# Moving activation tiles by 32 to 192 bytes against the weights in SBUF, in a chain of nine blocks whose matmuls read float32r operands

## The chip, the core and the metric

The kernel runs on one NeuronCore of one Trainium2 chip. The metric is the device time of one execution in microseconds (us), the median of three runs.

## The reference

A sequence of 256 tokens of width 1024 goes through two layers of a first model and one layer of a second, all in float32:

```
for i in range(2):
    x = x + 0.5 * swiglu(rms_norm(x, ffn1_norm[i]), w_gate[i], w_up[i], w_down[i])   # width 2816
    h = rms_norm(x, mix_norm[i])
    x = x + (moba_mixer(h, ...) if i == 0 else mamba2_mixer(h, ...))
    x = x + 0.5 * swiglu(rms_norm(x, ffn2_norm[i]), w_gate2[i], w_up2[i], w_down2[i])

def swiglu(x, w_gate, w_up, w_down):
    return (jax.nn.silu(x @ w_gate) * (x @ w_up)) @ w_down

# second model
h = rms_norm_2(x, norm_g) * (1.0 + scale) + shift
proj = h @ w_in                        # 1024 x 9216, then two gated recurrences
x = x + gate * (m @ w_out)
return rms_norm_2(x, final_g)
```

Almost all of the work is a product of 256 tokens with weight matrices that are read once.

## The kernel before

Every weight matrix comes in units of 128 x 2048 float32 (8 KB in each of 128 partitions). A ring of three slots, `raw`, takes them from HBM. ScalarE copies a unit to `w_hi` as float32r (`split_hi`, L390), and VectorE writes the rest, raw minus `w_hi`, to `w_lo` (`split_lo`, L402). Activations are split in the same way. A product is then three float32r matmuls into one accumulator: activation hi by weight hi, activation hi by weight lo, activation lo by weight hi. The units follow one another in one order through all stages, and semaphores (`hi_ready`, `lo_ready`, `unit_used`) hand the slots on.

A matmul on TensorE has two operands in SBUF. The stationary one (128 x 128) is loaded into the array first, with an instruction of its own in the trace (LDWEIGHTS, engine PEld), and the moving one (128 x 256 or 128 x 512) streams through it. The load for the next matmul runs while the present one streams.

- In the four feed-forward blocks, gate and up (L705, L712, L718) have the normed input `hT` as the stationary operand and `w_hi` or `w_lo` as the moving one. Down (L735 to L737, L750 to L752) has the hidden activations as the stationary operand: `hidT_hi` and `hidT_lo` for chunks with an even number, `odd_hidT_hi` and `odd_hidT_lo` for odd ones.
- The projections of attention (L438, L439, L445), of the z part of the second mixer (L1510 to L1512) and most of those of the second model (L2003 to L2005) also hold `hT` and move the weights.
- Where the output is wanted turned, the weights are the stationary operand and `hT` moves, 256 columns wide (L473, L475, L481, L509) or 512 (L504, L1462).
- The three output projections hold `oT`, `yT` and `mT` (L1159 to L1163, L438 to L445, L2031 to L2053). Their tiles lie in the work region and keep their distance from the weights modulo 256 bytes.

Tiles get their addresses by hand. `keep` puts one tile behind the other from the start of SBUF, each rounded up to 64 bytes, and `region` gives a second allocator that starts at a given offset:

```
x = keep("x", [P, TT, D])
hT = keep("hT", [P, KD, 2, SEQ], R32)
...
WORK = -(-top[0] // 128) * 128
```

Within the tiles all steps between operands are multiples of 512 bytes (a tile `hT[:, k, part, t*128:...]` starts at 2048 k + 1024 part + 512 t), but for L1462, whose stationary tiles are 256 bytes apart.

Of the kernel before, what the change touches and what calls it, by code (L numbers as in the profile page):

```python
# [144 lines left out]
def build(nc, w, out):  # L145
    with ExitStack() as ctx:
# [19 lines left out]
        top = [-(-nc.sbuf_base // 64) * 64]  # L166

        def at(offset, name, shape, dt=F32):
            t = nc.alloc_sbuf_tensor_at(name, shape, dt, offset=offset)
            size = int(np.prod(shape[1:])) * 4  # L170
            assert offset + size <= nc.sbuf_usable_end, (name, offset + size - nc.sbuf_usable_end)
            return t, offset + -(-size // 64) * 64

        def keep(name, shape, dt=F32):
            t, top[0] = at(top[0], name, shape, dt)
            return t

        def region(start):

            end = [start]  # L180

            def take(name, shape, dt=F32):
                t, end[0] = at(end[0], name, shape, dt)
                return t

            return take, end

        x = keep("x", [P, TT, D])
        hT = keep("hT", [P, KD, 2, SEQ], R32)
        hT_hi, hT_lo = hT[:, :, 0, :], hT[:, :, 1, :]  # L190
        raw = keep("raw", [P, SLOTS, UNIT])
        w_hi = keep("w_hi", [P, SLOTS, UNIT], R32)
# [1 line left out]
        ffn_tiles = top[0]  # L194
        silu_g = keep("silu_g", [P, TT, FC])
        hid = keep("hid", [P, TT, FC])
        hidT_hi = keep("hidT_hi", [P, 2, SEQ], R32)
        hidT_lo = keep("hidT_lo", [P, 2, SEQ], R32)
        const1 = keep("const1", [P, FIRST_W])
        cols = keep("cols", [P, P])  # L200
        taps = keep("taps", [P, P])
# [10 lines left out]
        WORK = -(-top[0] // 128) * 128  # L212
# [12 lines left out]


        start, start_end = region(WORK + 8192)
        rows_in = start("rows_in", [P, P])
        taps_in = start("taps_in", [P, P])
# [4 lines left out]
        trig = start("trig", [P, 2, TT, HALF])  # L234

        norm, _ = region(WORK)
        xn = norm("xn", [P, TT, D])
        ffn, _ = region(WORK + 7 * 8192)
        hidT = ffn("hidT", [P, 2, SEQ])
        hidT_parts = ((hidT_hi, hidT_lo), (ffn("odd_hidT_hi", [P, 2, SEQ], R32), ffn("odd_hidT_lo", [P, 2, SEQ], R32)))  # L240


# [8 lines left out]
        late, _ = region(late_start)  # L251
# [38 lines left out]
        head_rows, _ = at(r2_end[0] - 4 * SEQ, "head_rows", [P, SEQ])  # L290
        step_rows, _ = at(r2_end[0] - 8 * SEQ, "step_rows", [2 * SH, 2 * SEQ])
# [2417 lines left out]
```

How the kernel before makes its waits and increments, by code:

```python
            def order(*instructions):  # L158
                for i in instructions:
                    i.then_inc(sem(name), 1)
                counts[name] = counts.get(name, 0) + len(instructions)
                engine.wait_ge(sem(name), counts[name])
# [205 lines left out]
        def load_unit(sp, unit, halves, step=0, per=0):  # L368
            n, slot, turn = place(unit, step, per)
            if unit >= SLOTS:
                sp.wait_ge(sem("lo_ready"), n - (SLOTS - 1))
            for dst, src in halves:
                sp.dma_start(dst, src).then_inc(sem(f"landed_{slot}"), 16)
# [5 lines left out]
        def split_hi(act, unit, step=0, per=0):  # L379
            if unit >= UNITS:
                return
            n, slot, turn = place(unit, step, per)
            act.wait_ge(sem(f"landed_{slot}"), 16 * PARTS * (turn + 1))
            if unit >= SLOTS:
                act.wait_ge(sem("unit_used"), n - (SLOTS - 1))
            to, src = w_hi[:, slot, :], raw[:, slot, :]
            if unit == FIRST_UNIT["ssm_dt"]:
                to, src = (step_weights(part, slot)[:, :, 0:SH] for part in (w_hi, raw))
            act.activation(to, src, ACT.Copy).then_inc(sem("hi_ready"), 1)
# [1 line left out]
        def split_lo(dve, unit, step=0, per=0):  # L392
            if unit >= UNITS:
                return
            n, slot, _ = place(unit, step, per)
            dve.wait_ge(sem("hi_ready"), n + 1)
            to, src, hi = w_lo[:, slot, :], raw[:, slot, :], w_hi[:, slot, :]
            if unit == FIRST_UNIT["ssm_dt"]:
```

## Time and profile before

| what | value |
| --- | --- |
| time, median of 3 runs | 1321.93 us (1321.92 to 1321.98) |
| the profiled execution's own time | 1321.68 us |
| its span, first to last instruction | 1319.9 us |
| TensorE busy | 1308.6 us, 99% of the span |
| VectorE busy | 1079.1 us, 82% |
| ScalarE busy | 713.6 us, 54% |
| matmuls | 7751 |
| moved from HBM | 252 MB, 192 GB/s over the span |

The busy time of a matmul in the trace runs from its start to its modelled end, and matmuls overlap in it: the mean of 389 ns for one is not what it costs in a stream. What it costs is the distance between the starts of two that follow one another, and that is read from the timeline.

### The profile page before, as it was taken

The numbers are of one execution on the slowest core, as the hardware profiler recorded it, in microseconds if no ns is written. First come the engines' busy times: TensorE is split into PE (matmuls) and PEld (weight loads), VectorE is DVE, ScalarE is ACT, GpSimd is POOL, SyncE is SP. The second block draws the span as 40 slices with busy tenths as digits, with TensorE's granted clock in tenths as the row PEclk, the third lists the DMA queues.
The fourth block names the chain that finished last, engine by engine and source line by source line (L and its number), as shares of the span: only waits on it lengthen the run. The fifth ranks groups of instructions, "written<-read, shape, count | busy, mean of one in ns | idle before, by whom it ended". The sixth has DMA issues, their size and how long they took to land.

```text
span 1319.9 us, 20183 instructions
## 1 busy us (share of the span) xinstructions
PE 1308.6 (99%) x7751; PEld 1105.4 (84%) x7751; DVE 1079.1 (82%) x1592; ACT 713.6 (54%) x840; POOL 205.1 (16%) x193
## 2 busy tenths in 40 slices
PE   9999999999999999999999999999999999999998
PEld 7888888888888888888899988888888888888886
DVE  6977788868999789998786999769777767878587
ACT  6444455665444454444465688854444466558553
POOL 2400001102000010000000035200000001654940
PEclk9999999999999999999999999999999999999999
DMA  8655556528577654876544565475655555654541
GB/s 274 223 191 191 191 179 204 191 77 306 192 260 267 242 186 146 269 233 222 184 160 155 175 215 180 145 257 166 210 194 196 197 171 160 200 172 143 175 152 56
DMA packets 158445, 254.29 MB, mean 193 GB/s; under 512 B 8800, under 2 KB 99248, under 8 KB 156704
## 3 DMA queue, kind: packets, MB, share of 16 engines
q1 hardware_dynamic: 155136, 232.68, 53.0%
q0 software_dynamic: 2576, 18.45, 4.0%
q10 hardware_dynamic: 656, 2.11, 0.4%
q8 instruction: 52, 0.85, 0.3%
q14 instruction: 25, 0.20, 0.0%
HBM read 252.12 MB, written 1.08 MB: 192 GB/s over the span
## 4 chain that ended last, share of the span: by engine, by line
PE 97%; DVE 1%; issue 1%; ACT 1%; DMA 0%; SPq 0%; POOLq 0%; POOL 0%; DVEq 0%; ACTq 0%
PE psum L718 12%; PE psum L712 12%; PE psum L705 12%; PE psum L736 6%; PE psum L737 5%; PE psum L735 5%; PE psum L2003 4%; PE psum L2004 4%; PE psum L2005 4%; PE psum L438 3%; PE psum L439 3%; PE psum L445 3%; PE psum L473 2%; PE psum L481 2%; PE psum L475 2%; PE psum L504 2%
## 5 line engine op out<-in xcount | busy, mean ns | idle before, releaser
L390 ACT ACTIVATE w_hi<-raw 128x2048 fp32r<-128x2048 f32 (+1 forms) x220 | 419.7, 1910 | 316.5 <-PE psum L718 121.0
L402 DVE TENSOR_TENSOR w_lo<-raw,w_hi 128x2048 fp32r<-128x2048 f32 x219 | 506.8, 2335 | 99.7 <-ACT w_hi L390 98.2
L839 DVE STREAM_TRANSPOSE hidT<-hid 32x128 f32<-32x128 f32 x704 | 213.2, 303 | 22.1
L705 PE MATMUL psum<-w_hi,hT 128*128 128x512 f32 x704 | 174.5, 390 | 0.1
L718 PE MATMUL psum<-w_lo,hT 128*128 128x512 f32 x704 | 173.9, 389 | 0.0
L712 PE MATMUL psum<-w_hi,hT 128*128 128x512 f32 x704 | 173.9, 389 | 0.0
L705 PEld LDWEIGHTS psum<-w_hi,hT 128*128 128x128 f32 x704 | 131.8, 188 | 27.9 <-ACT w_hi L1009 0.8
L712 PEld LDWEIGHTS psum<-w_hi,hT 128*128 128x128 f32 x704 | 132.1, 188 | 27.5
L718 PEld LDWEIGHTS psum<-w_lo,hT 128*128 128x128 f32 x704 | 132.1, 188 | 27.4
L786 ACT ACTIVATE silu_g<-psum,rstd 128x256 f32<-128x256 f32 x88 | 37.0, 472 | 113.5 <-PE psum L718 107.9
L2003 PE MATMUL psum<-w_hi,hT 128*128 128x512 f32 x224 | 88.7, 396 | 0.0
L2005 PE MATMUL psum<-w_hi,hT 128*128 128x512 f32 x224 | 87.3, 390 | 0.0
L2004 PE MATMUL psum<-w_lo,hT 128*128 128x512 f32 x224 | 87.3, 390 | 0.0
L473 PE MATMUL psum<-hT,w_hi 128*128 128x256 f32 x256 | 62.6, 285 | 0.0
L737 PE MATMUL psum<-w_hi,odd_hidT_lo 128*128 128x512 f32 x160 | 62.2, 389 | 0.0
L735 PE MATMUL psum<-w_hi,hidT_hi 128*128 128x512 f32 x160 | 62.2, 389 | 0.0
L736 PE MATMUL psum<-w_lo,hidT_hi 128*128 128x512 f32 x160 | 62.2, 389 | 0.0
L737 PE MATMUL psum<-w_hi,hidT_lo 128*128 128x512 f32 x160 | 62.2, 389 | 0.0
L735 PE MATMUL psum<-w_hi,odd_hidT_hi 128*128 128x512 f32 x160 | 62.2, 389 | 0.0
L736 PE MATMUL psum<-w_lo,odd_hidT_hi 128*128 128x512 f32 x160 | 62.2, 389 | 0.0
L475 PE MATMUL psum<-hT,w_lo 128*128 128x256 f32 x256 | 62.1, 283 | 0.0
L830 DVE TENSOR_TENSOR hid<-psum,silu_g 128x512 f32<-128x512 f32 x44 | 30.3, 689 | 36.9 <-ACT silu_g L786 36.9
(407 smaller groups left out, 2180.6 us busy)
## 6 DMA issues: line engine op xcount, KB each, us to landing
raw<-in_ffn_w_down SPq DMA_DIRECT2D x88, 512.0 KB, 5.2
raw<-in_ffn_w_gate SPq DMA_DIRECT2D x87, 512.0 KB, 4.1
raw<-in_ffn_w_up SPq DMA_DIRECT2D x87, 512.0 KB, 5.3
raw<-in_w_in SPq DMA_DIRECT2D x72, 512.0 KB, 4.6
raw<-in_ssm_w_in SPq DMA_DIRECT2D x48, 512.0 KB, 4.6
raw<-in_attn_w_qkv SPq DMA_DIRECT2D x24, 512.0 KB, 4.8
ada_in<-in_w_ada POOLq DMA_DIRECT2D x8, 1536.0 KB, 7.2
raw<-in_ssm_w_out SPq DMA_DIRECT2D x16, 512.0 KB, 4.4
```

The source lines that it names most:

```text
L390: act.activation(to, src, ACT.Copy).then_inc(sem("hi_ready"), 1)
L402: dve.tensor_tensor(to, src, hi.bitcast(F32), ALU.subtract).then_inc(sem("lo_ready"), 1)
L705: pe.matmul(psum[:, banks[t], :], hT_hi[:, k, t * P:(t + 1) * P], hi[:, kk, :], start=k == 0, stop=False)
L712: pe.matmul(psum[:, banks[t], :], hT_lo[:, k, t * P:(t + 1) * P], hi[:, kk, :], start=False, stop=False)
L718: m = pe.matmul(psum[:, banks[t], :], hT_hi[:, k, t * P:(t + 1) * P], lo[:, kk, :], start=False, stop=k == KD - 1)
L735: pe.matmul(to, a, hi[:, k, cs], start=start and k == 0, stop=False)
L736: pe.matmul(to, a, lo[:, k, cs], start=False, stop=False)
L737: m = pe.matmul(to, b, hi[:, k, cs], start=False, stop=False)
L839: dve.transpose(to[:, :, :, 32 * a:32 * (a + 1)], src[:, :, :, 32 * b:32 * (b + 1)])\
L2003: pe.matmul(to, a, hi[:, kk, :], start=k == 0, stop=False)
L2004: pe.matmul(to, a, lo[:, kk, :], start=False, stop=False)
L2005: m = pe.matmul(to, b, hi[:, kk, :], start=False, stop=k == KD - 1)
```

## The change

The change moves no instruction and no wait: on each of the five engines the instructions before and after are the same and in the same order. Only addresses differ. Three gaps are put between tiles that stand one behind the other, and one in the work region (`skip` is new and raises the allocator's top):

```
+        def skip(size):
+            top[0] += size
+
...
         x = keep("x", [P, TT, D])
+        skip(64)
         hT = keep("hT", [P, KD, 2, SEQ], R32)
+        skip(192)
         hT_hi, hT_lo = hT[:, :, 0, :], hT[:, :, 1, :]
         raw = keep("raw", [P, SLOTS, UNIT])
         w_hi = keep("w_hi", [P, SLOTS, UNIT], R32)
...
         hid = keep("hid", [P, TT, FC])
+        skip(32)
         hidT_hi = keep("hidT_hi", [P, 2, SEQ], R32)
         hidT_lo = keep("hidT_lo", [P, 2, SEQ], R32)
+        skip(224)
         const1 = keep("const1", [P, FIRST_W])
...
-        ffn, _ = region(WORK + 7 * 8192)
+        ffn, ffn_end = region(WORK + 7 * 8192)
         hidT = ffn("hidT", [P, 2, SEQ])
+        ffn_end[0] += 192
         hidT_parts = ((hidT_hi, hidT_lo), (ffn("odd_hidT_hi", [P, 2, SEQ], R32), ffn("odd_hidT_lo", [P, 2, SEQ], R32)))
```

The byte offsets in a partition that the two kernels give these tiles, and where each then stands against the weights (start of the tile minus start of `w_hi`, modulo 256):

| tile | offset before | offset after | against the weights before | after |
| --- | --- | --- | --- | --- |
| `hT` | 24704 | 24768 | 0 | 64 |
| `w_hi` | 65664 | 65920 | - | - |
| `w_lo` | 90240 | 90496 | 0 | 0 |
| `hidT_hi` | 118912 | 119200 | 0 | 32 |
| `hidT_lo` | 120960 | 121248 | 0 | 32 |
| `odd_hidT_hi` | 191104 | 191808 | 0 | 192 |
| `odd_hidT_lo` | 193152 | 193856 | 0 | 192 |
| `oT`, `yT`, `mT` (work region) | from 131712 | from 132224 | 0 | 0 |

Before, all of these start at 128 modulo 512. The gaps that follow each moved tile fill up to 256 bytes, so that everything behind it, the work region too, stands where it did modulo 256.

## Rows read from the trace of the kernel before

**Rows 1.** the profile's page, parts 1 and 2: busy time, and the granted clock
```profile
PE 1308.6 (99%) x7751; PEld 1105.4 (84%) x7751; DVE 1079.1 (82%) x1592; ACT 713.6 (54%) x840; POOL 205.1 (16%) x193
...
PEclk9999999999999999999999999999999999999999
```

**Rows 2.** the page, part 4: the chain that ended last
```profile
PE 97%; DVE 1%; issue 1%; ACT 1%; DMA 0%; SPq 0%; POOLq 0%; POOL 0%; DVEq 0%; ACTq 0%
```

**Rows 3.** waits of TensorE: total us, times, longest
```profile
PE psum L978 <- DVE hidT_lo L1034: 1.4, 1, 1.4
PE psum L504 <- DVE hT L2509: 0.9, 1, 0.9
```

**Rows 4.** groups by line and shape: count | busy us, mean ns | idle before
```profile
L705 PE MATMUL psum<-w_hi,hT 128*128 128x512 f32 x704 | 174.5, 390 | 0.1
...
L473 PE MATMUL psum<-hT,w_hi 128*128 128x256 f32 x256 | 62.6, 285 | 0.0
```

**Rows 5.** Instructions on hT, hidT_hi, hidT_lo, odd_hidT_hi, odd_hidT_lo, in turn (xcount)
```profile
0.00:1320.00 1320.00, 906.23 (x4344) 752.03 (x4344) 24.96 (x60) 23.01 (x60) 1.00 0.58 193
...
0.00:1320.00 1320.00, 118.34 (x384) 72.00 (x384) 16.44 (x24) 14.81 (x24) 1.00 0.58 193
...
0.00:1320.00 1320.00, 82.05 (x214) 41.34 (x214) 16.93 (x25) 1.00 0.58 193
...
0.00:1320.00 1320.00, 98.54 (x320) 60.05 (x320) 13.92 (x20) 12.32 (x20) 1.00 0.58 193
...
0.00:1320.00 1320.00, 62.25 (x160) 30.04 (x160) 13.92 (x20) 1.00 0.58 193
```

**Rows 6.** Timeline of TensorE, gate and up: start us, us, instruction
```profile
15.12 1.98 PE L705 MATMUL psum<-w_hi,hT 128*128 128x512 f32 x8
...
29.63 0.62 PE L718 MATMUL psum<-w_lo,hT 128*128 128x512 f32 x2
```

**Rows 7.** Timeline of TensorE, a turned projection, 256 columns
```profile
663.66 0.28 PE L475 MATMUL psum<-hT,w_lo 128*128 128x256 f32 x1
...
667.13 1.12 PE L481 MATMUL psum<-hT,w_hi 128*128 128x256 f32 x8
```

**Rows 8.** Timeline of TensorE, the start
```profile
1.45 4.36 PE L978 MATMUL psum<-hidT_lo 128*128 128x512 f32 x10 [1.45 <-DVE hidT_lo L1034]
5.74 0.23 PE L985 MATMUL psum<-const,rows_in 16*128 16x16 f32 x1
...
11.46 2.01 PE L712 MATMUL psum<-w_hi,hT 128*128 128x512 f32 x8
13.31 1.98 PE L718 MATMUL psum<-w_lo,hT 128*128 128x512 f32 x8
```

**Rows 9.** Timeline of TensorE, attention: float32 operands, 256 columns
```profile
254.44 0.60 PE L1190 MATMUL psum<-qkT 128*128 128x256 f32 x2
254.87 0.59 PE L1199 MATMUL psum<-probT,v_sb 128*128 128x256 f32 x2
255.31 0.38 PE L1200 MATMUL psum<-probT,v_sb 128*128 128x128 f32 x2
```

**Rows 10.** Timeline of TensorE after transposes, at two places
```profile
297.27 2.07 PE L705 MATMUL psum<-w_hi,hT 128*128 128x512 f32 x8
299.18 1.98 PE L712 MATMUL psum<-w_hi,hT 128*128 128x512 f32 x8
...
724.27 2.08 PE L1462 MATMUL psum<-hT,w_hi 128*128 128x512 f32 x8
726.19 0.28 PE L473 MATMUL psum<-hT,w_hi 128*128 128x256 f32 x1
```

**Rows 11.** Busy us of engines by stage: PE, PEld, DVE, ACT, POOL
```profile
296.00:476.00 180.00, 179.99 (x801) 149.02 (x800) 161.04 (x255) 84.34 (x84) 11.56 (x12) 1.00 0.71 248
...
745.00:835.00 90.00, 88.80 (x799) 76.98 (x798) 83.99 (x156) 70.76 (x122) 34.26 (x42) 1.00 0.55 188
```

More of the change, by code:

```diff
@@ L176, in keep, with skip @@
             return t
+        def skip(size):
+            top[0] += size
         def region(start):
@@ L188, in build @@
         x = keep("x", [P, TT, D])
+        skip(64)
         hT = keep("hT", [P, KD, 2, SEQ], R32)
+        skip(192)
         hT_hi, hT_lo = hT[:, :, 0, :], hT[:, :, 1, :]
@@ L196, in build @@
         hid = keep("hid", [P, TT, FC])
+        skip(32)
         hidT_hi = keep("hidT_hi", [P, 2, SEQ], R32)
         hidT_lo = keep("hidT_lo", [P, 2, SEQ], R32)
+        skip(224)
         const1 = keep("const1", [P, FIRST_W])
@@ L237, in build @@
         xn = norm("xn", [P, TT, D])
-        ffn, _ = region(WORK + 7 * 8192)
+        ffn, ffn_end = region(WORK + 7 * 8192)
         hidT = ffn("hidT", [P, 2, SEQ])
+        ffn_end[0] += 192
         hidT_parts = ((hidT_hi, hidT_lo), (ffn("odd_hidT_hi", [P, 2, SEQ], R32), ffn("odd_hidT_lo", [P, 2, SEQ], R32)))
```

## The prediction

> **What bounds the kernel now.** I read the page's busy times first: TensorE is busy for 99% of the span, VectorE for 82%, ScalarE for 54%, and the granted clock stands at its full level of 2.4 GHz in every slice [rows 1]. The chain that ended last says the same: 97% of it is TensorE [rows 2]. The waits confirm that nothing holds TensorE up: its two longest are 1.4 us at the very start and 0.9 us at the head of the second model [rows 3]. So the time is the number of matmuls times what each costs in a stream, and other engines and DMA matter only if TensorE gets quicker than they can feed it.
>
> What one costs does not stand in the groups. Their mean of 390 ns for 512 columns and 285 ns for 256 [rows 4] includes overlap with the next. The starts tell it. In gate and up, eight groups of eight matmuls start between 15.12 and 29.63 us [rows 6]: 14.51 us over 64 is 226.7 ns for 512 columns. In a turned projection 29 matmuls of 256 columns start between 663.66 and 667.13 us [rows 7]: 119.7 ns. Two sizes give a line: (226.7 - 119.7) / 256 = 0.418 ns for a column and a fixed part of 12.7 ns for each matmul, whatever its length. The column price is one column for each cycle of 2.4 GHz, and no address changes that. The fixed part, 5.6% of a 512-column matmul, is what the change can reach.
>
> **Is the fixed part a matter of addresses?** Three groups bear on it.
>
> First, it is smaller where the moving operand is read at half the rate. The first ten matmuls of the program, with the same operand shapes, take 5.74 - 1.45 = 4.29 us [rows 8], 429 ns each with the slow first one in it; that is two times 512 x 0.418 = 428 ns, so they ran at 1.2 GHz, before TensorE had been at work, and leave about 1 ns for a fixed part. In attention the operands are plain float32, and four matmuls of 256 columns take 255.31 - 254.44 = 0.87 us [rows 9], 217.5 ns each: two passes of 256 x 0.418 = 214 ns, and 3.5 ns more. A fixed part that came from exchanging the weights in the array would have shown in both. One that comes from two SBUF reads that get in each other's way at full rate (512 columns streaming, while the next 128 x 128 is loaded) would be just what shows.
>
> Second, it is not constant at the same addresses. After a disturbance eight matmuls take longer: 13.31 - 11.46 = 1.85 us for eight, 231 ns each [rows 8]. There is then a small, repeatable stretch of odd distances before they settle at 226.7. So the fixed part depends on how the two streams stand to each other in time. The distance in address would be another way to shift one against the other.
>
> Third, a shift of 256 bytes does nothing. L1462 has every second stationary tile 256 bytes off the moving one. Its eight matmuls after a block of transposes take 726.19 - 724.27 = 1.92 us, and eight of gate and up after a block of transposes, all at distance 0, take 299.18 - 297.27 = 1.91 us [rows 10]. If addresses count at all, they count modulo 256 or less. No row shows a distance other than 0 modulo 256, so the price of the new ones, 64, 32 and 192, has to be bounded.
>
> **The change, part by part.** It adds and removes no instruction, no DMA and no wait, so nothing is queued differently. The matmuls whose two operands move against each other are those with `hT` (4344), `hidT_hi` (384), `hidT_lo` (214, less the 22 warm-up ones that have it on both sides) and the two odd tiles (320 and 160) [rows 5]: 4344 + 384 + 192 + 320 + 160 = 5400. `oT`, `yT` and `mT` keep their distance, as do float32 operands. VectorE and ScalarE read and write the moved tiles as well. `hT` takes only 24.96 us of VectorE's time and 23.01 us of ScalarE's [rows 5], which TensorE's work covers; I cost their new addresses at nothing. Uncovered, a tenth more on both would be 5 us.
>
> The bounds for one matmul: at best the fixed part drops to the 3.5 ns of the float32 rows, a gain of 9.2 ns, or to the 1 ns of the first ten, 11.7 ns. At worst it becomes that of the disturbed eight, 231.2 - 226.7 = 4.5 ns lost. Times 5400 these are 50 us gained (63 at the outermost) and 24 us lost. In between I take half of the 9.2 ns, 4.6 ns: three different distances are used, and nothing says that all are equally good. That is 5400 x 4.6 ns = 25 us.
>
> Can the others follow? In the second feed-forward block, the tightest of the four, VectorE is busy for 161 of 180 us [rows 11]. Half the gain takes 801 x 4.6 ns = 3.7 us off the 180, all of it 7.4 us, and 161 still fits in 172.6. In the stage from 745 to 835 us VectorE has 84 of 90, but most of TensorE's 799 instructions there are float32 ones that the change leaves alone. I take off nothing for it in the middle case, and 2 us from the full gain.
>
> The Trainium skill has a rule that speaks against the change. In "SBUF — State Buffer", section "Who interferes with whom", TensorE has two independent read ports, one for the moving operand and one for the weight load, and never waits on anyone. By it the load takes nothing from the stream and the time stays as it is. The fixed part that is absent at half rate speaks against the rule; no row tests it at another address. The page "TensorE: Matmul & The Clock Gate", section "Back-to-back issue gap", gives columns / 2.4 + 2.5 ns for an isolated matmul; if every moved one came down to that, an estimate of the gain is 5400 x 10.3 ns = 56 us.
>
> **The rivals.**
> - *All of it goes.* Any distance other than 0 keeps the streams apart: 5400 x 9.2 = 50 us, less 2, gives 1321.7 - 48 = 1274 us. For it: the half-rate rows have hardly any fixed part. Against: the streams run at different speeds past each other, so that a shift may only move the place at which they meet.
> - *Addresses don't count.* The fixed part is one of TensorE's own, tied to time and rate: 1322 us. For it: the 256-byte shift that did nothing, and the same 226.7 ns in every stage. Against: only the untested distances could tell.
> - *The new distances are worse.* At 64 bytes the moving stream, twice as fast as the load, meets it more often, as in the disturbed eight: 1321.7 + 24 = 1346 us. It decides from the point at which a settled matmul on `hT`, 4344 of the 5400, takes over 227 ns. For it: almost all disturbed distances are above 226.7, so the settled one seems a good case.
>
> **How the numbers follow.** The profiled execution took 1321.68 us, the median of the runs is 1321.93; I subtract from the first and let the 0.25 us go. Part of the fixed part goes: 1321.7 - 25 = 1297 us, chance 0.33, own range 1282 to 1316. All of it goes: 0.17. Addresses don't count: 0.28. Worse: 0.22. About 0.2% (2.6 us) is what a measurement of this kernel can tell from no change, so faster has 0.50, same 0.28, slower 0.22. The range reaches from 1266, inside the full gain with its price read a little too small, to 1340, which leaves out the upper third of the worse case.
>
> **What the changed profile would show.** Right: the starts of L705, L712 and L718 less than 226.7 ns apart in settled stretches, some 222; a turned projection at 115 instead of 119.7; TensorE still at 99%; output projections (`yT`, `oT`, `mT`) unchanged at 226.7, as the control. Even and odd down projections (L735 to L737) may differ, and show which distance is the better. Wrong: the same 226.7 everywhere (addresses don't count), more than that (worse), or a faster TensorE that now waits for `lo_ready` from VectorE (the gain eaten by the split of the weights).

## The result and the profile after

The changed kernel takes 1344.97 us (median of 4 runs, 1344.54 to 1346.18), the kernel before 1321.93: a ratio of 1.0174, interval 1.0161 to 1.0187. It is 23 us slower, and the experiments below show that the distances chosen make it so.

The page of the changed kernel, parts 1, 2 and 4, reads like that of before [rows 1, 2]: the same instructions, TensorE busy for 99% at the full granted clock (2.4 GHz), VectorE no busier.

```profile
span 1343.4 us, 20183 instructions
...
PE 1332.3 (99%) x7751; PEld 1103.3 (82%) x7751; DVE 1076.8 (80%) x1592; ACT 712.8 (53%) x840; POOL 205.3 (15%) x193
...
PEclk9999999999999999999999999999999999999999
...
PE 97%; DVE 1%; issue 1%; ACT 1%; DMA 0%; SPq 0%; POOLq 0%; POOL 0%; DVEq 0%; ACTq 0%
```

The waits of TensorE are those of before [rows 3] too, so no engine holds it up:

```profile
PE psum L986 <- DVE hidT_lo L1042: 1.4, 1, 1.4
PE psum L512 <- DVE hT L2517: 0.9, 1, 0.9
```

The 23.5 us between the two spans have to lie in the distances between matmul starts. Here is the timeline of TensorE in the same stretch of gate and up as in [rows 6] (start us, us, instruction; line numbers are 8 higher than before):

```profile
15.08 2.03 PE L713 MATMUL psum<-w_hi,hT 128*128 128x512 f32 x8
...
28.14 2.03 PE L720 MATMUL psum<-w_hi,hT 128*128 128x512 f32 x8
```

From 15.08 to 28.14 us lie seven groups of eight: 13.06 us over 56 is 233.2 ns, where [rows 6] gives 226.7. One by one, the starts stand 231 and 236 ns apart in turn, through the whole of this stretch. In other stretches of the same trace they stand 233 and 234 ns apart; both patterns average 233.3. Down, in the first even chunk and in the first odd one (one row for each third matmul, 24 in all to the next L713):

```profile
43.08 0.40 PE L743 MATMUL psum<-w_hi,hidT_hi 128*128 128x512 f32 x1
...
48.67 2.03 PE L713 MATMUL psum<-w_hi,hT 128*128 128x512 f32 x8
...
59.87 0.39 PE L743 MATMUL psum<-w_hi,odd_hidT_hi 128*128 128x512 f32 x1
...
65.37 2.03 PE L713 MATMUL psum<-w_hi,hT 128*128 128x512 f32 x8
```

The even one, at distance 32, takes 5.59 us over 24 or 232.9 ns each, the odd one, at 192, 5.50 us or 229.2 ns. The turned projection, where `hT` moves 256 columns, got quicker. 20 matmuls lie between these two starts, 2.36 us or 118.0 ns each, against 119.7 in [rows 7]:

```profile
680.66 0.28 PE L481 MATMUL psum<-hT,w_hi 128*128 128x256 f32 x1
...
683.02 0.75 PE L489 MATMUL psum<-hT,w_hi 128*128 128x256 f32 x5
```

With the distances from each matmul's start to the next summed over the whole trace, the 23.5 us come out in full (the differences are those of the sums before rounding):

| matmuls | count | before, us | after, us | difference |
| --- | --- | --- | --- | --- |
| hold `hT`, move weights, 512 columns | 3312 | 756.8 | 777.6 | +20.7 |
| hold even hidden tiles | 576 | 130.7 | 134.5 | +3.8 |
| hold odd hidden tiles | 480 | 108.8 | 110.2 | +1.3 |
| hold weights, move `hT`, 256 columns | 896 | 108.0 | 105.9 | -2.1 |
| hold weights, move `hT`, 512 columns | 136 | 31.3 | 31.5 | +0.1 |
| hold `oT`, `yT`, `mT`, not moved against the weights | 359 | 78.0 | 78.0 | +0.1 |
| all others | 1991 | 98.0 | 97.6 | -0.4 |

### The profile page after: what moved, and what is told of

Its sections match the earlier page's. It is cut to its first block, busy times and chain, and to the rows that moved or that the text cites. A ratio compares the mean times of both kernels' runs of the same rounds, so it can differ in the third digit from the quotient of the medians.

```text
span 1343.4 us, 20183 instructions
## 1 busy us (share of the span) xinstructions
PE 1332.3 (99%) x7751; PEld 1103.3 (82%) x7751; DVE 1076.8 (80%) x1592; ACT 712.8 (53%) x840; POOL 205.3 (15%) x193
## 4 chain that ended last, share of the span: by engine, by line
PE 97%; DVE 1%; issue 1%; ACT 1%; DMA 0%; SPq 0%; POOLq 0%; POOL 0%; DVEq 0%; ACTq 0%
PE psum L726 12%; PE psum L720 12%; PE psum L713 12%; PE psum L745 6%; PE psum L744 6%; PE psum L743 5%; PE psum L2011 4%; PE psum L2012 4%; PE psum L2013 4%; PE psum L446 3%; PE psum L453 3%; PE psum L447 3%; PE psum L481 2%; PE psum L489 2%; PE psum L483 2%; PE psum L512 2%
## 5 line engine op out<-in xcount | busy, mean ns | idle before, releaser
L410 DVE TENSOR_TENSOR w_lo<-raw,w_hi 128x2048 fp32r<-128x2048 f32 x219 | 504.3, 2324 | 113.0 <-ACT w_hi L398 111.7
L713 PE MATMUL psum<-w_hi,hT 128*128 128x512 f32 x704 | 179.1, 396 | 0.1
L726 PE MATMUL psum<-w_lo,hT 128*128 128x512 f32 x704 | 178.5, 395 | 0.0
L720 PE MATMUL psum<-w_hi,hT 128*128 128x512 f32 x704 | 178.5, 395 | 0.0
L713 PEld LDWEIGHTS psum<-w_hi,hT 128*128 128x128 f32 x704 | 131.7, 188 | 32.3 <-ACT w_hi L1017 0.8
L2011 PE MATMUL psum<-w_hi,hT 128*128 128x512 f32 x224 | 89.9, 401 | 0.0
L2012 PE MATMUL psum<-w_lo,hT 128*128 128x512 f32 x224 | 88.5, 395 | 0.0
L2013 PE MATMUL psum<-w_hi,hT 128*128 128x512 f32 x224 | 88.5, 395 | 0.0
```

The source lines that it names most:

```text
L410: dve.tensor_tensor(to, src, hi.bitcast(F32), ALU.subtract).then_inc(sem("lo_ready"), 1)
L713: pe.matmul(psum[:, banks[t], :], hT_hi[:, k, t * P:(t + 1) * P], hi[:, kk, :], start=k == 0, stop=False)
L720: pe.matmul(psum[:, banks[t], :], hT_lo[:, k, t * P:(t + 1) * P], hi[:, kk, :], start=False, stop=False)
L726: m = pe.matmul(psum[:, banks[t], :], hT_hi[:, k, t * P:(t + 1) * P], lo[:, kk, :], start=False, stop=k == KD - 1)
L2011: pe.matmul(to, a, hi[:, kk, :], start=k == 0, stop=False)
L2012: pe.matmul(to, a, lo[:, kk, :], start=False, stop=False)
```

## The experiments

**Theory and rivals.** A: the distance modulo 256 between what a matmul holds and what it moves sets how the weight load and the stream get in each other's way, and so the pace that a stream of float32r matmuls settles at. B: the absolute address of the held tile does it. C: it comes from the writes that ScalarE and VectorE make beside TensorE. D: the part of 13 ns is the exchange of weights in the array, and distance acts on something else.

**One, the cost by itself.** A kernel with TensorE alone; it and the three others of its kind below ran once each. Two tiles are filled from x; 48 matmuls a group at one distance, the held tile stepping by 512 bytes and the moved one by 1024; a plain float32 matmul ahead of each group.

```
for a, b, n in GROUPS:                  # bytes held, bytes moved, columns
    mark(pe)                            # plain float32, L50
    for i in range(48):
        s, m = a // 4 + 128 * (i % 8), b // 4 + 256 * (i // 2 % 4)
        pe.matmul(psum[:, i % 2, 0:n], held[:, s:s + 128], moved[:, m:m + n], ...)
```

> This kernel leaves out the whole model: TensorE alone, on operands copied from x, in groups of 48 float32r matmuls at a chosen distance between the stationary and the moving operand, a plain float32 matmul ahead of each group; the output is x. Theory A (the distance modulo 256 decides how the weight load and the stream collide): 226.7 ns a matmul of 512 columns at distance 0 and 256, 233.3 ns at 32, 64 and 320, the same 226.7 where both operands are shifted by 64 or by 32, and something else again at other distances, some perhaps under 226.7. Theory B (the absolute address of the stationary operand decides, wherever the moving one lies): both shifted by 64 gives 233.3, and a shift of the moving operand alone gives 226.7. Theory C (the loss of the changed kernel comes from what ScalarE and VectorE do beside TensorE): 226.7 in every group, since nothing runs beside it.

Its timeline; the L62 rows are the groups at distance 0, at 64, moved alone by 64 (held minus moved -64, which is 192), and both by 64:

```profile
20.71 11.18 PE L62 MATMUL psum<-moved,held 128*128 128x512 f32 x48
31.73 0.38 PE L50 MATMUL psum<-x 128*128 128x128 f32 x2
...
66.13 11.45 PE L62 MATMUL psum<-moved,held 128*128 128x512 f32 x48
77.42 0.38 PE L50 MATMUL psum<-x 128*128 128x128 f32 x2
...
258.80 11.25 PE L62 MATMUL psum<-moved,held 128*128 128x512 f32 x48
269.89 0.38 PE L50 MATMUL psum<-x 128*128 128x128 f32 x2
...
281.44 11.14 PE L62 MATMUL psum<-moved,held 128*128 128x512 f32 x48
292.42 0.38 PE L50 MATMUL psum<-x 128*128 128x128 f32 x2
```

A group lasts from its start to the L50 row behind it: 11.02 us at distance 0, 11.29 at 64, 11.09 and 10.98 for the other two. The passage after the L50 is in these; the mean over the last 24 starts of a group is the settled pace:

| held minus moved, bytes | 512 columns, ns | 256 columns, ns |
| --- | --- | --- |
| 0, 256 | 226.7 | 120.0 (at 0) |
| 32 | 233.3 | 118.3 |
| 64, 320 | 233.3 | 117.8 (at 64) |
| 96 | 234.2 | 117.5 |
| 128 | 232.8 | 118.8 |
| 160 | 233.3 | 120.0 |
| 192 | 228.9 | 117.8 |
| 224 | 233.3 | 116.7 |
| both shifted by 64, or both by 32 | 226.7 | |
| moved alone by 64 (distance 192), by 192 (distance 64) | 228.9, 233.3 | |

These are the paces of the kernel: 233.3 in gate and up, 118 where `hT` moves. B and C fall here: both operands shifted together change nothing, the moved one shifted alone does, and nothing ran beside TensorE.

**Two and three, half of the change each.** `hT` alone is shifted (the gaps around the hidden tiles and the one in the work region set to 0), and the hidden tiles alone (the gaps around `hT` set to 0).

```
         x = keep("x", [P, TT, D])
-        skip(64)
+        skip(0)          # hidden tiles alone, and so the 192 behind hT; in the other kernel both stay
...
-        skip(32)
+        skip(0)          # hT alone, and so the 224 behind them; in the other kernel both stay
...
-        ffn_end[0] += 192
+        ffn_end[0] += 0  # hT alone
```

> hT alone 64 bytes off the weights, the hidden tiles at distance 0 again. Theory A: 3312 matmuls that hold hT pay 6.6 ns more each, 21.9 us, and 896 that move it in 256 columns gain 2 ns each, 1.8 us: 1322 + 20 = 1342 us, with the down projections back at 226.7 ns. Theory C: no sum of the parts, since the other engines' writes of hT are only 48 us long; anything else than 1342.

> The hidden tiles alone are shifted (even 32, odd 192), hT at distance 0. Theory A: 576 matmuls at distance 32 pay 6.6 ns more, 3.8 us, and 480 at distance 192 pay what the changed kernel shows there, 2.8 ns on average, or nothing if that was only the passage from the state that the gate and up matmuls leave: 1322 + 4 to 5 = 1326 to 1327 us. Gate and up back at 226.7 ns. Theory C: gate and up stay slow as well.

`hT` alone: 1340.02 us, ratio 1.0139 (1.0122 to 1.0156). Its 3312 holding matmuls sum to 777.3 us, as in the changed kernel; the down projections, at distance 0 again, keep 227.8 and 227.6 ns on average instead of 226.9 and 226.7, 0.5 us each. The hidden tiles alone: 1326.73 us, ratio 1.0037 (1.0023 to 1.0051), with 757.4 us for the holding ones, 134.4 for the even and 109.9 for the odd. The two losses, 18.3 and 5.0 us, add to the whole of 23. The second is the 1326 to 1327 us expected; the first is 2 us less than expected, since the 3312 lost 20.5 us and not 21.9, and the 896 turned ones gained 3.0 and not 1.8. The odd tiles' 229.0 ns is no passage that gate and up leave: it stays when those are at 226.7, and the sweep has 228.9 at distance 192.

**Four, every distance.** The first kernel with 64 distances, 0 to 252 in steps of 4, 512 columns.

> The model is left out again: TensorE alone, 48 float32r matmuls of 512 columns at every distance from 0 to 252 bytes in steps of 4, the output is x. Theory A1 (the settled pace is a property of the whole pattern of collisions, and the 226.7 ns of distance 0 and 144 is its floor): no distance under 226.7 ns, most between 230 and 234. Theory A2 (somewhere the two streams miss each other altogether): a few distances near 216 to 222 ns, which a multiple of 16 bytes doesn't reach.

Settled paces over the 64 distances: 226.7 ns at six (0, 120, 132, 156, 216, 240), 228.9 to 232.2 at 19, 233.3 or 233.4 at 33, up to 236.7 at six. The mean is 232.2. None is under 226.7. So A1 holds and A2 falls: for 512 columns and 128 held ones distance 0 is already on the floor, and most of what one could pick is 3 to 7 ns worse. At 144 bytes the first sweep had settled at 226.7 and this one did at 233.3.

**Five, what the effect needs.** Other shapes and types at distances 0, 32, 64, 144 and 192, in the same way.

```
tiles = {"r": (held, moved, 4), "b": (held_b, moved_b, 2), "f": (held_f, moved_f, 4)}   # float32r, bfloat16, float32
pe.matmul(psum[0:width, bank, 0:n], h[:, s:s + width], v[:, m:m + n], ...)
```

> The model is left out: TensorE alone, distances 0, 32, 64, 144 and 192 bytes for other shapes and types; the output is x. Theory A (weight load and stream read SBUF in each other's way when the stream reads 4 bytes a column at full rate): plain float32 of 256 columns near 216 ns and bfloat16 near 216 ns for 512 columns at every distance, float32r depending on the distance at 384 columns too, and with 64 or 32 stationary columns a smaller fixed part than 13 ns, since the load is shorter. Rival D (the fixed part is the exchange of weights in the array and the distance acts on something else): the same 13 ns with 64 and 32 stationary columns and with bfloat16.

The timeline at distances 0 and 64, for float32 (each matmul is two instructions there) and for bfloat16:

```profile
216.74 20.89 PE L71 MATMUL psum<-moved_f,held_f 128*128 128x256 f32 x96
...
258.62 20.89 PE L71 MATMUL psum<-moved_f,held_f 128*128 128x256 f32 x96
...
321.67 10.31 PE L71 MATMUL psum<-moved_b,held_b 128*128 128x512 bf16 x47
...
342.83 10.31 PE L71 MATMUL psum<-moved_b,held_b 128*128 128x512 bf16 x47
```

Float32 and bfloat16 don't care: 215.8 ns for one float32 instruction of 256 columns and for 512 columns of bfloat16, at all five distances, and 109.2 for 256 columns of bfloat16. Float32r does at 384 columns (173.3 at four distances, 176.7 at 64) and no longer at 128 (111.7 everywhere). But with 64 or 32 held columns the fixed part did not shrink: 228.3 to 233.3 and 231.0 to 240.0 ns, though the load's own rows in the trace fell from 192 ns to 134 and 108. That part of A's expectation failed. Distance 0 is not the best there either: with 64 held columns it takes 230.0 and 192 takes 228.3, with 32 it takes 231.7 and 144 takes 231.0. D fails as well: bfloat16 has 2.5 ns beyond its columns and not 13, and with fewer held columns the part is not the same. So among the streams tried only float32r, with 4 bytes a column at full rate, shows the effect; that it grows with the length of the load is not so.

**Six, from the sweep to the kernel.** All moved tiles at 192.

```
         skip(64)                       # before hT
         hT = keep("hT", [P, KD, 2, SEQ], R32)
-        skip(192)                      # behind it: hT stays, the weights come 128 bytes nearer
+        skip(64)
...
-        skip(32)                       # before hidT_hi
+        skip(192)
...
-        skip(224)                      # behind hidT_lo
+        skip(64)
```

> hT, the even and the odd hidden tiles all at distance 192. If the paces of the sweep (TensorE alone) hold in the kernel, 4368 matmuls that hold a shifted tile cost 228.9 ns and not 226.7, 9.6 us; 896 that move hT in 256 columns, now at distance 64 the other way, cost 117.8 and not 120.0, 1.9 us less; 136 of 512 columns cost 233.3, 0.9 us more: 1321.7 + 8.6 = 1330 us. If the changed kernel is slow for another reason (three distances side by side, or writes by other engines), nothing ties the time to this sum.

1327.71 us, ratio 1.0044 (1.0028 to 1.0061), where the sum from the sweep said 1330; the profiled execution took 1328.58. Timeline of gate and up:

```profile
15.00 2.00 PE L713 MATMUL psum<-w_hi,hT 128*128 128x512 f32 x8
...
27.82 1.99 PE L720 MATMUL psum<-w_hi,hT 128*128 128x512 f32 x8
```

12.82 us over 56 is 228.9 ns, the sweep's pace at 192. The 512-column matmuls that move `hT` went from 230.4 to 234.8 ns on average. The difference to the sum is mostly in the turned matmuls, which took 117.0 ns on average rather than 117.8 and had 120.5 before, 3.2 us gained instead of 1.9. They have a second settled pattern that no group of the sweep shows. Between these two rows lie 77 starts, 8.72 us or 113 ns each:

```profile
704.98 0.28 PE L483 MATMUL psum<-hT,w_lo 128*128 128x256 f32 x1
...
713.70 1.98 PE L489 MATMUL psum<-hT,w_hi 128*128 128x256 f32 x16
```

In all, 303 of the 896 turned matmuls stand 113 or 114 ns from the next here, 254 with `hT` alone at 64 (190 of them in one stretch), 64 in the changed kernel and 10 before. Most of the others take 117 to 119. So two paces exist at one distance in one kernel, and this is why the turned matmuls gained 3.0 us with `hT` alone and 2.1 in the changed kernel. What picks the pattern is not shown.

**Seven, what stands beside what.** TensorE alone, offsets that alternate between two values, fewer columns, and some distances repeated.

```
GROUPS = [(0, 0, 0, 0, 512), (0, 64, 0, 64, 512), (64, 0, 0, 64, 512), ...]   # held even, held odd, moved even, moved odd
```

> The model is left out: TensorE alone, 48 matmuls a group, the output is x. First part, offsets that alternate from one matmul to the next. Theory A3 (the load for the next matmul and the present stream get in each other's way): with both operands of every second matmul shifted by 64 or 32, so that a matmul's own two stand at distance 0 but each load at plus or minus 64 from the stream it lies beside, the pace leaves 226.7; with held and moved shifted in turn, so that each load stands at 0 from the stream beside it while a matmul's own two are at 64, it is 226.7. Theory A4 (a matmul's own two operands count): the other way round. Second part, 480 to 508 columns at distance 0: if the settled pace can only stand at steps of 6.67 ns (16 columns), 496 columns give 220.0 and 500 to 508 give 220 to 226.7 in means that are fractions of 6.67 over a repeating pattern; if it is a fixed 13.3 ns, each 4 columns give 1.67 ns. Third part, distance 144 and 240 several times over: 226.7 at some and 233.3 at others means that more than one settled pattern exists at one distance.

With each matmul's own operands at distance 0 and the load beside a stream at plus or minus 64: 231.7 ns (for 32 also). With the load at 0 to the stream beside it and a matmul's own operands at plus or minus 64: 233.3 (for 32: 230.0). Neither A3 nor A4 alone gives this; both pairings cost. Fewer columns at distance 0: 508 take 227.8, more than 512; 504 and 500 take the same 226.7 as 512, 496 take 223.3, 492 take 220.0, and 488 take 226.0, more than 492. So it is no constant 13.3 ns on top of the columns, and it is not the simple step either, by which 496 would have taken 220.0.

The order of the distances depends on the width too, and within a few columns:

| columns | distance 0, ns | distance 64, ns |
| --- | --- | --- |
| 512 | 226.7 | 233.3 |
| 508 | 227.8 | 229.2 |
| 504 | 226.7 | 228.9 |
| 496 | 223.3 | 220.0 |
| 480 | 216.7 | 215.9 |

At 496 and 480 columns the shifted operands are the quicker ones. Every settled pattern of float32r whose length I worked out sums to a multiple of 6.67 ns (226.7 is 34 of them, 231 + 236 is 70; a steady 230.0 needs two, 69). Distance 144 settled at 233.3 five times out of five, and 240 at 228.3, 226.7 and 228.3: more than one pattern exists at one distance. What picks it was not varied by itself.

**Eight, the absolute address.** Before's kernel, all tiles 64 bytes further on.

```
-        top = [-(-nc.sbuf_base // 64) * 64]
+        top = [-(-nc.sbuf_base // 64) * 64 + 64]
...
-        WORK = -(-top[0] // 128) * 128
+        WORK = top[0]
```

> Every tile of the kernel of before, weights, activations, constants and work region, 64 bytes further on: hT stands at the absolute address that the changed kernel gives it, at distance 0 from the weights. Theory A (distance): 1321.7 us, within 0.2%, and 226.7 ns in gate and up. Rival B (absolute address of hT): about 1342 us, as with hT alone shifted.

1321.56 us, ratio 1.0000 (0.9990 to 1.0009). `hT` stands where the changed kernel has it, and the pace is that of before, 14.51 us over 64 matmuls:

```profile
15.02 1.98 PE L705 MATMUL psum<-w_hi,hT 128*128 128x512 f32 x8
...
29.53 0.84 PE L718 MATMUL psum<-w_lo,hT 128*128 128x512 f32 x3
```

**Nine, only where it pays.** `hT` is kept at distance 0, but for the second mixer, where it is mostly the moved operand; all tiles behind it move by 256 bytes.

```
         hT = keep("hT", [P, KD, 2, SEQ], R32)
+        top[0] += 256
+        further_hT = nc.alloc_sbuf_tensor_at("further_hT", [P, KD, 2, SEQ], R32, offset=hT_at + 192)
...
+            use_hT(further_hT)         # on GpSimd, ScalarE, VectorE, TensorE alike
             ssm_pe(pe)
+            use_hT(plain_hT)
```

> The kernel of before, with hT 192 bytes further on in the second mixer alone, where 768 matmuls move it in 256 columns and 192 hold it. By the all_192 run the 768 take 90.3 us instead of 92.7 and the 192 holding ones 45.8 instead of 45.1: 1.7 us gained, 1320.0 us, 0.13%, at the edge of what can be told. If the passage between the stages costs more than that, 1322 us.

1320.07 us, as expected, ratio 0.9987 (0.9978 to 0.9996), 1.6 us below before and so the quickest of all versions, by an amount that the interval only just separates from none. The turned matmuls sum to 105.6 us instead of 108.0, 192 of them again at 113 or 114 ns; those that hold `hT` to 757.7 instead of 756.8. In the first unit 29 starts lie between these two rows, 3.42 us or 117.9 ns each:

```profile
663.37 0.28 PE L484 MATMUL psum<-further_hT,w_lo 128*128 128x256 f32 x1
...
666.79 1.46 PE L490 MATMUL psum<-further_hT,w_hi 128*128 128x256 f32 x11
```

## Why the prediction was wrong

*What bounds the kernel* was right: TensorE's pace at 226.7 and 119.7 ns, and all the rest hidden. Waits and the other engines did not change.

*Is the fixed part a matter of addresses?* The answer, yes, modulo 256 or less, was right. It rested on the missing fixed part in [rows 8, 9], on the restless stretch after a disturbance in [rows 8] and on the 256-byte shift in [rows 10]; the sweeps show all three again (215.8 ns for float32, 226.7 at distance 256, and at distance 0 a mean of 232.2 over the first 24 distances of a group before it settles). Two readings were weaker than they looked. The "about 1 ns" of the first ten is a mean of a slow first one (591 ns), seven at 426 or 427 and two short ones (385 and 328); the seven, 512 columns at half the pace, leave nothing. Their pace of 1.2 GHz was read from these distances, where the granted clock of the stretch stands at 1.00. And both stretches of [rows 10] were still unsettled behind their first matmul (224 to 236 and 226 to 232 ns), so they could not have told a few nanoseconds.

*The bounds and the value between them* is the step that failed: "In between I take half of the 9.2 ns". It supposed that distance 0 is a bad or a middling case, from which another distance leads to the 3.5 ns of the float32 rows. The sweep of 64 distances shows 226.7 as the lowest settled pace there is, reached at six. The gain bound was not open at all: float32's small fixed part is there at all five distances tried, so it does not come from how its operands stand. Nor is it the slower stream alone: bfloat16, a column in each cycle like float32r but with half the bytes, has 2.5 ns too. And the upper bound was too low. I took the 231.2 ns of eight disturbed matmuls [rows 8], 4.5 ns lost; the settled paces at 64 and at 32 are 233.3, 6.6 ns lost, for 3312 and 576 matmuls.

*One sign for all 5400* was wrong too. 896 of them move `hT` in 256 columns, and those gained 2.1 us. Distance 0 is at 120.0 the worst of eight there, level with 160. The odd hidden tiles, at 192, lost 2.2 ns at the settled pace, a third of what 32 and 64 cost.

*The rival "the new distances are worse"* had the right sign and, at 1346 us, the right size, but by two errors that cancel: its 4.5 ns is too small, and it charges it to the turned matmuls as well. With what was measured the sum is 20.7 + 3.8 + 1.3 - 2.1 + 0.1 + 0.1 - 0.4 = 23.5 us. Its argument, that almost all disturbed distances are above 226.7 so that the settled one seems a good case, was the evidence in the trace, and it deserved more than 0.22. Had I asked where in the spread of these numbers the settled one lies, instead of how far it lies from an ideal, the forecast would have been slower for 512 columns. For 256 the same question points the other way, as the runs did: the first three distances in the stretch of [rows 7], before it settles at 120, are 121, 116 and 118.

*The rule of two independent read ports* in the Trainium skill, "SBUF — State Buffer", section "Who interferes with whom", was taken to mean no change. For float32r that does not come out: held and moved operand shifted against each other by 64 bytes cost 6.6 ns a matmul, and shifted together nothing. Whether it is at the ports that they meet, the runs don't show. For bfloat16 and float32 nothing here contradicts the rule. The 2.5 ns that the Trainium skill gives for an isolated matmul, in "TensorE: Matmul & The Clock Gate", section "Back-to-back issue gap", agree with bfloat16 here, though each matmul has a load of its own: 215.8 ns for 512 columns. They agree with no float32r group of 512.

*Expected in the changed profile*: the control came out (`oT`, `yT`, `mT` unchanged in sum), and even and odd chunks did show which distance is the better of the two, 192. The starts of 512 columns under 226.7 did not, and the turned projection went to 118, not 115.

What stays open: why the load and the stream settle where they do. The nine kernels show which distances cost what, that the settled patterns sum to multiples of 6.67 ns, and that the paces at distance 0 and 64 depend neither on absolute addresses nor on other engines. They don't show the mechanism: that the load and the stream get in each other's way is still a theory, the fixed part does not follow the number of held columns, and both pairings tried in the seventh experiment cost. The multiple of 6.67 ns was read from the patterns, not caused and taken away.

## What to carry to other kernels

In a stream of float32r matmuls with 128 held columns and 512 moved ones, place the held tiles and the moved ones at the same offset modulo 256 bytes, and check it after every change of the allocator: a gap of 32 or 64 bytes costs 6.6 ns for each matmul, 3%, without a trace in waits or in busy shares. The distance between starts is where it shows; measure it for a few distances in a kernel of TensorE alone, for the widths that the kernel uses, before moving a tile, since other widths want other distances: at 256, 480 and 496 columns distance 64 was quicker than 0. When a quantity varies by itself in a trace, ask where its settled value lies within that variation before hoping to better it.

## What the runs showed that I had not expected

- Float32r has a pace of its own: 226.7 ns for 512 columns at the best of 64 distances, where bfloat16 takes 215.8, and the fixed part does not shrink with fewer held columns.
- 500, 504 and 512 columns cost the same 226.7 ns at distance 0, and 488 cost more (226.0) than 492 (220.0). At 496 columns distance 64 takes 220.0 ns and distance 0 takes 223.3, the reverse of 512.
- One distance can have several settled patterns: 144 bytes gave 226.7 ns in one kernel and 233.3 in two others, 240 bytes both 226.7 and 228.3 in one. In the whole kernel the turned matmuls ran at some 118 ns in one stretch and at 113 in another, at one distance.
